# The third pair of gate units by seven products, with h's two parts added on GpSimd

## What is computed

```
h = rms_norm(x);  z = h @ w_in          # gate_logits: 3 x 1024 columns of z
y_rnn = (rg_lru(x_rnn) * silu(g_rnn)) @ rg_out
y_sc  = (short gated convolution) @ sc_out
y_att = (latent attention * silu(g_att)) @ mla_out
gates = sigmoid(gate_logits + gate_b)   # three branches
merged = gates[0] * y_rnn + gates[1] * y_sc + gates[2] * y_att
x = x + merged @ w_out
```

## Time and profile before

| | |
|---|---|
| three runs | 1686.08, 1681.82, 1685.59 us; median 1685.59 |
| profiled execution | 1684.07 us, its span 1682.3 us, clock granted 0.999 |
| PE busy | 1667.4 us (99%) |
| DVE busy | 1130.8 us (67%) |
| ACT busy | 579.8 us (34%) |
| POOL busy | 1252.7 us (74%) |

### The profile page before, as it was taken

How to read it: one execution, slowest core, us unless ns; L and a number is a source line. 1 busy time by engine, 2 the same in 40 slices (tenths; PEclk the granted TensorE clock), 3 DMA queues, 4 the chain that set the end, 5 groups by cost and what they waited for, 6 DMA issues and landing times.

```text
span 1682.3 us, 31902 instructions
## 1 busy us (share of the span) xinstructions
PE 1667.4 (99%) x11840; PEld 1566.7 (93%) x11840; DVE 1130.8 (67%) x1563; ACT 579.8 (34%) x1037; POOL 1252.7 (74%) x1345
## 2 busy tenths in 40 slices
PE   7999999999999999999999999999999999999999
PEld 7999999999999999999998888888888888899887
DVE  7965748485566687777349657484846666978751
ACT  5423333242344323433135233333323343234320
POOL 7764848385888787898866748484867996899983
PEclk9999999999999999999999999999999999999999
DMA  4431213222322223332532312221322323333333
GB/s 156 144 103 62 95 61 94 67 81 90 99 89 87 87 89 101 115 128 85 165 118 77 112 60 97 66 89 67 94 92 84 100 87 101 88 126 117 122 101 115
DMA packets 50295, 164.50 MB, mean 98 GB/s; under 512 B 6144, under 2 KB 7552, under 8 KB 50176
## 3 DMA queue, kind: packets, MB, share of 16 engines
q1 hardware_dynamic: 42192, 146.56, 27.4%
q10 hardware_dynamic: 8032, 17.00, 2.9%
HBM read 152.21 MB, written 10.81 MB: 97 GB/s over the span
## 4 chain that ended last, share of the span: by engine, by line
PE 90%; DVE 6%; issue 2%; ACT 1%; ACTq 0%; POOL 0%; DVEq 0%; POOLq 0%
PE slots L628 69%; PE slots L901 10%; PE slots L693 3%; PE slots L727 3%; PE slots L789 2%; PE slots L711 1%; DVE early L1534 1%; DVE early L1549 1%; PE slots L662 1%; DVE qr_hi_and_lo L1366 1%; PE slots L678 1%; DVE kr_lo L1366 1%; DVE kn_lo L1366 1%; DVE weight_sums L1808 0%; DVE early L1556 0%
## 5 line engine op out<-in xcount | busy, mean ns | idle before, releaser
L491 POOL TENSOR_TENSOR w_lo<-w_raw,w_hi 128x256 fp32r<-128x256 f32 x860 | 753.1, 905 | 17.9
L486 POOL TENSOR_SCALAR w_hi<-w_raw 128x1024 fp32r<-128x1024 f32 x215 | 260.5, 1212 | 217.7 <-PE slots L628 205.5
L628 PE MATMUL slots<-h_hi,w_hi 128*128 128x264 f32 (+1 forms) x1680 | 405.3, 308 | 0.7 <-DVE sc_pad L1662 0.7
L628 PE MATMUL slots<-h_lo,w_hi 128*128 128x264 f32 (+1 forms) x1680 | 399.9, 305 | 0.0
L628 PE MATMUL slots<-h_hi,w_lo 128*128 128x264 f32 (+1 forms) x1680 | 399.5, 304 | 0.0
L628 PEld LDWEIGHTS slots<-h_hi,w_hi 128*128 128x128 f32 x1680 | 270.9, 188 | 14.8 <-issue 1.6
L628 PEld LDWEIGHTS slots<-h_hi,w_lo 128*128 128x128 f32 x1680 | 270.1, 188 | 12.9
L628 PEld LDWEIGHTS slots<-h_lo,w_hi 128*128 128x128 f32 x1680 | 270.3, 188 | 12.1
L628 PE MATMUL slots<-branch_hi,w_hi 128*128 128x264 f32 (+1 forms) x552 | 143.8, 320 | 9.2 <-DVE branch_lo L1379 8.5
L628 PE MATMUL slots<-branch_lo,w_hi 128*128 128x264 f32 (+1 forms) x552 | 142.4, 317 | 0.0
L628 PE MATMUL slots<-branch_hi,w_lo 128*128 128x264 f32 (+1 forms) x552 | 142.0, 317 | 0.0
(11 more groups left out here) (276 smaller groups left out, 3695.9 us busy)
## 6 DMA issues: line engine op xcount, KB each, us to landing
w_raw<-w_units SPq DMA_DIRECT2D x251, 512.0 KB, 3.5
stream<-sc_acc ACTq DMA_DIRECT2D x16, 264.0 KB, 2.1
sc_back<-stream SPq DMA_DIRECT2D x8, 528.0 KB, 3.6
x_old<-stream SPq DMA_DIRECT2D x16, 264.0 KB, 4.7
stream<-residual_or_merged ACTq DMA_DIRECT2D x16, 264.0 KB, 2.7
ab_raw<-w_units SPq DMA_DIRECT2D x8, 512.0 KB, 4.1
residual_or_merged<-xt ACTq DMA_DIRECT2D x4, 528.0 KB, 7.5
stream<-xt ACTq DMA_DIRECT2D x1, 2112.0 KB, 9.5
```

Source lines behind the costliest of these rows:

```text
L486: pool.tensor_scalar(hi, raw, 1.0, 1.0, ALU.mult, ALU.mult).then_inc(sem("hi_part"), 1)
L491: op = pool.tensor_tensor(lo[:, cols], raw[:, cols], hi[:, cols].bitcast(F32), ALU.subtract)
L628: mm = pe.matmul(out[:, a_, 0:t1 - t0], w(k), x(k)[:, t0:t1], start=(n == 0), stop=(n == 3 * ks - 1))
```

## The change

PLAIN becomes 2, so gate pair 2 (turn 1 of MR, the attention gate), the third, goes by seven products; the number of such pairs in a layer rises from 9 to 10. The additions of h's two parts move from DVE to POOL: two after the split of pair 0 (chunks 0 and 1) and two after that of y0's unit (chunks 2 and 3), with waits of their own on the end of the recurrence's readers. ACT's order puts mix_upper(2) ahead of gates(1), mix_upper(3) behind it, and drops gates(2). DVE's order makes the mixes earlier: att_gate(0) behind mixes_lower(1), and merge(0, 0) behind the weight sums. merge(0, 1) and att_gate(1) come from the loop over pairs, around the third pair's sums.

```diff
-PLAIN = 3
+PLAIN = 2
@@ POOL
+                def whole_h(i):
+
+                    pool.wait_ge(*at("rg_mm", l, 3, 4))
+                    pool.wait_ge(*at("in_x", l, 3, 2))
+                    if i > 1:
+                        pool.wait_ge(*at("rnn_full", l, 3, i - 1))
+                    for n in range(2):
+                        pool.tensor_tensor(tile(mix_whole, i)[:, n * T:(n + 1) * T], tile(h_hi, i + 4 * n).bitcast(F32),
+                                           tile(h_lo, i + 4 * n).bitcast(F32), ALU.add).then_inc(sem("h_again"), 1)
+
                 split_pair(0)
+                whole_h(0)
+                whole_h(1)
                 for i in range(4):
                     split_unit("MR", l, i, 2, 2)
                     if i:
                         branch_lower(i - 1)
+                    else:
+                        whole_h(2)
+                        whole_h(3)
                     split_pair(2 * i + 1)
@@ ACT
                 gates(0)
                 mix_upper(0)
                 mix_upper(1)
-                gates(1)
                 branch_upper(0)
                 mix_upper(2)
+                gates(1)
                 mix_upper(3)
-                gates(2)
                 for n in range(4):
                     lead_upper(0, n)
@@ DVE, in mixes(i)
-                    for n in range(2):
-                        dve.tensor_tensor(whole[:, n * T:(n + 1) * T], tile(h_hi, i + 4 * n).bitcast(F32),
-                                          tile(h_lo, i + 4 * n).bitcast(F32), ALU.add).then_inc(sem("h_again"), 1)
                     dve.wait_ge(*at("h_again", l, i, 2))
@@ DVE
                 mixes(0)
                 mixes(1)
+                mixes_lower(0)
+                mixes(2)
+                mixes_lower(1)
                 att_gate(0)
-                mixes_lower(0)
-                mixes_lower(1)
-                mixes(2)
+                mixes(3)
+                mixes_lower(2)
+                weight_sums(0)
                 merge("MR", 0, 0)
-                mixes_lower(2)
-                merge("MR", 0, 1)
-                mixes(3)
-                weight_sums(0)
                 mixes_lower(3)
-                att_gate(1)
```

## The result

The changed kernel takes 1688.77 us (median of 9 runs, 1686.63 to 1689.99), the kernel before beside it 1684.73 us (9 runs, 1681.82 to 1686.08). The ratio is 1.0028, 95% interval 1.0019 to 1.0037: slower by 0.28%, about 4 us, where 2.2 us of gain were forecast. The time lies inside the range given, on the wrong side of the kernel before.

A forecast was written before the change was run, and what follows sets the result against it. PE's own work was taken as the bound: 2.74 us less for the third pair, 0.5 us of waiting for its leads, nothing for additions and mixes, so 1685.59 became 1683.3 us; range 1679.8 to 1689.5.

The follow-up runs named there:

- e1: The kernel before, third pair still plain, with only the additions of h's two parts moved to POOL: 1685.88 us, ratio 1.0003.
- e12: The kernel before with ScalarE making four ring units' upper halves, unit 1/2's ahead of the fourth mixture's upper half: 1684.57 us, ratio 0.9998.
- e4: The changed kernel with lead uppers ahead of mix_upper(3), last lower half ahead of merge(0, 0), branch_lower(0) behind the fourth pair's leads: 1694.9 us, ratio 1.0058.
- e7: The changed kernel with POOL's branch_lower(0) ahead of the third pair's leads: 1690.0 us, ratio 1.0033.
- e11: The changed kernel with ScalarE making four ring units' upper halves, branch_lower(0) ahead of the third pair's leads, additions back on DVE: 1685.97 us, ratio 1.001.
- e5: The changed kernel with ScalarE instead of POOL making the upper halves of four ring units per layer: 1684.68 us, ratio 0.9999.
- e8: The changed kernel with only ACT's four lead uppers moved ahead of the mixes' upper half of chunk 3: 1688.63 us, ratio 1.0022.

## What to carry to other kernels

Where two engines exclude each other, add up the work of both between the last release and the deadline; moving the additions from one to the other freed nothing that the runs show (three pairs of kernels, 1.4, 0.3 and 0.1 us apart, none with the advantage of POOL shown), and only work given to a third engine did (4 us). Idle time of the one engine is then not free for filling while the other's chain is late. And if a stage is brought forward by one step, reckon the step behind it again: its inputs can now meet what the earlier one pushed back.

## Not expected of the hardware

**Stretches at the lower clock after a long pause of PE, and behind one-column matmuls.** Far from the change, the profile after has PE at the lower level for 3.5 us, a few us behind 16 matmuls of 128x1 (timeline, then the window; in the window's row the third number from the end is the granted clock):

```profile
898.45 1.95 PE L783 MATMUL slots<-ones,early 128*128 128x1 f32 x16
...
902.44 0.41 PE L804 MATMUL slots<-w_hi,kv_hi 128*128 128x256 f32 x1
```

```profile
900.00:906.00 6.00, 6.00 (x39) 6.00 (x39) 5.48 (x11) 2.53 (x3) 5.87 (x7) 0.72 0.34 112
```

A matmul of 256 columns starts every 0.21 us there and every 0.12 before and behind, half the rate: the 1.2 GHz level. The profile before has 1.00 in the same window and 52 matmuls in it instead of 39. It has the same 16 matmuls, so they alone don't decide it, and what does stays open. It isn't the change's doing either: the profiles of e1 and e12, whose third pair is plain, show 0.72 and 0.73 in that window, those of e4, e7 and e11, with the third pair by seven products, 1.00. Whole runs differ in the same way: of the kernel before's 28 runs beside e5 to e8 11 had a mean clock of 0.998 (mean 1686.17 us), 16 of 0.999 (1684.27) and one of 1.000 (1683.38). Of the changed kernel's 9 runs 6 had 0.998 (mean 1689.13), 2 had 0.999 (1688.07) and one 1.000 (1686.63). At equal clock the changed kernel is thus 3 to 4 us slower, which the waits of the two pairs explain.

The kernel with the leads ahead shows the same behind a pause. After PE had waited 3.25 us at 1461.31 (its third pair in layer 1 took 15.90 us):

```profile
1454.00:1462.00 8.00, 4.75 (x33) 4.34 (x32) 7.86 (x9) 3.12 (x5) 8.00 (x7) 0.89 0.24 75
1462.00:1470.00 8.00, 8.00 (x51) 8.00 (x50) 5.62 (x8) 1.42 (x3) 7.92 (x9) 0.69 0.37 123
1470.00:1476.00 6.00, 6.00 (x32) 5.05 (x32) 5.79 (x9) 1.64 (x3) 3.34 (x3) 1.00 0.30 90
```

9.88 us and about 3.5 of waiting leave some 2.5 us for the lower clock. The waits of 0.57 and 1.33 us in the changed kernel had no such stretch behind them, so in these two executions two short waits came cheaper than the one long one that replaced them; the medians (+4.0 and +3.9 us) don't show it.
